# Differential attention: 24 projection pieces in the first 16 steps, score tiles three ahead from step 20

## What is computed

```
q, k, v = split(x @ w_qkv)                 # per head: two queries and keys of 64, a value of 128
q, k = partial_rotary(q) * 64 ** -.5, partial_rotary(k)
s = einsum('bqhcd,bkhcd->bhcqk', q, k)     # c = 0, 1; masked by chunks of 64
p = softmax(s)
a = p[:, :, 0] - lam * p[:, :, 1]
o = einsum('bhqk,bkhe->bqhe', a, v)
out = (rms_norm(o, g_sub) * (1 - lam_init)) @ w_o
```

## Time and profile before

| | |
|---|---|
| median of 3 runs | 2364.1 us (2362.1 to 2365.77) |
| the profiled execution | 2361.91 us, of which its span 2360.2 us |
| PE busy | 2289.7 us, 97% of the span |
| PE weight load, DVE, ACT, POOL busy | 83%, 54%, 43%, 33% |
| mean granted clock of PE | 0.995 |
| the attention loop, 32 steps | 1266.5 to 1410.7 us |

### The profile page before, as it was taken

One profiled execution on the slowest core, in us unless ns is written; L12 is line 12 of the kernel. 1 busy time (PEld: TensorE's weight loads), 2 busy tenths in 40 slices (PEclk: granted clock), 3 DMA queues, 4 the chain that ended last, 5 costly groups with the idle time before them and its releaser, 6 DMA issues. The chain is left out here.

```text
span 2360.2 us, 37346 instructions
## 1 busy us (share of the span) xinstructions
PE 2289.7 (97%) x14848; PEld 1954.7 (83%) x14848; DVE 1282.4 (54%) x2110; ACT 1020.1 (43%) x1690; POOL 775.0 (33%) x571
## 2 busy tenths in 40 slices
PE   9999999999999999999999989999999999999998
PEld 7877877878868878887887658999988888999986
DVE  6444246245635545544225774877754344777754
ACT  4345435143444543345434553554524323544522
POOL 3423344134420025333333413111254454111264
PEclk9999999999999999999999999999999999999999
DMA  5333222132210014432222212233223323233232
GB/s 153 72 72 72 82 90 89 36 81 77 89 54 3 3 38 98 90 72 54 83 89 72 72 37 72 90 107 107 93 105 106 107 89 108 90 108 107 89 107 89
DMA packets 137038, 191.96 MB, mean 81 GB/s; under 512 B 31024, under 2 KB 84656, under 8 KB 136896
## 3 DMA queue, kind: packets, MB, share of 16 engines
q1 hardware_dynamic: 128928, 183.64, 26.3%
q10 hardware_dynamic: 7968, 6.32, 0.9%
HBM read 187.84 MB, written 2.10 MB: 80 GB/s over the span
## 5 line engine op out<-in xcount | busy, mean ns | idle before, releaser
L823 POOL TENSOR_TENSOR weights_low<-weights_raw,weights_high 128x512 fp32r<-128x512 f32 x520 | 705.6, 1388 | 1205.6 <-ACT weights_high L1982 1205.6
L1982 ACT ACTIVATE weights_high<-weights_raw 128x1024 fp32r<-128x1024 f32 x260 | 260.9, 1050 | 384.3 <-PE bank L902 379.3
L900 PE MATMUL bank<-xt_high,weights_high 128*128 128x256 f32 (+1 forms) x1152 | 390.3, 339 | 3.9 <-ACT third_sum L2304 1.6
L902 PE MATMUL bank<-xt_high,weights_low 128*128 128x256 f32 (+1 forms) x1152 | 381.6, 331 | 0.0
L901 PE MATMUL bank<-xt_low,weights_high 128*128 128x256 f32 (+1 forms) x1152 | 381.0, 331 | 0.0
L900 PEld LDWEIGHTS bank<-xt_high,weights_high 128*128 128x128 f32 x1152 | 219.1, 190 | 30.7 <-POOL weights_low L823 4.9
L902 PEld LDWEIGHTS bank<-xt_high,weights_low 128*128 128x128 f32 x1152 | 218.9, 190 | 21.2
L901 PEld LDWEIGHTS bank<-xt_low,weights_high 128*128 128x128 f32 x1152 | 219.3, 190 | 16.6
L900 PE MATMUL bank<-weights_high,xt_high 128*128 128x512 f32 x432 | 173.7, 402 | 5.4 <-DVE xt_low L2869 2.8
L902 PE MATMUL bank<-weights_high,xt_low 128*128 128x512 f32 x432 | 168.8, 391 | 0.0
L901 PE MATMUL bank<-weights_low,xt_high 128*128 128x512 f32 x432 | 168.5, 390 | 0.0
(11 more groups left out here) (487 smaller groups left out, 4860.6 us busy)
## 6 DMA issues: line engine op xcount, KB each, us to landing
weights_raw<-in_fox_w_in_dram SPq DMA_DIRECT2D x64, 512.0 KB, 5.6
weights_raw<-in_ffn_w_gate_dram SPq DMA_DIRECT2D x44, 512.0 KB, 4.0
weights_raw<-in_ffn_w_up_dram SPq DMA_DIRECT2D x44, 512.0 KB, 5.0
weights_raw<-in_ffn_w_down_dram SPq DMA_DIRECT2D x40, 512.0 KB, 4.3
weights_raw<-in_gla_w_in_dram SPq DMA_DIRECT2D x24, 512.0 KB, 4.3
weights_raw<-in_gdn_w_in_dram SPq DMA_DIRECT2D x24, 512.0 KB, 4.5
weights_raw<-in_attn_w_qkv_dram SPq DMA_DIRECT2D x24, 512.0 KB, 4.5
weights_raw<-in_conv_w_in_dram SPq DMA_DIRECT2D x24, 512.0 KB, 4.3
```

The lines of the kernel that those rows point to most:

```text
L823: pool.tensor_tensor(w_lo[:, odd, k], raw[:, odd, k], w_hi[:, odd, k].bitcast(F32), ALU.subtract)\
L900: pe.matmul(out_ap, lh, rh, start=first, stop=False, skip_group_check=skip)
L902: return pe.matmul(out_ap, ll, rh, start=False, stop=last, skip_group_check=skip)
L1982: act.activation(w_hi[:, odd, 2 * m:2 * m + 2], raw[:, odd, 2 * m:2 * m + 2], ACT.Copy)\
```

## The change

The 24 pieces are dealt out anew: step n gets pieces 3n/2 to 3(n+1)/2 (rounded down), so even steps 0 to 14 have one, odd steps 1 to 15 have two, and steps 16 to 31 none. The first piece of a step stays ahead of the turning, a second one stands between the turning and the scores. `DEEP` goes from 26 to 20: step 18 issues the scores of 20 and 21, later steps are three ahead. ACT's copies and conversions and DVE's rotations follow the pieces, one step behind as before; with two pieces in a step they are done in the order of the pieces. ACT's copy of a head's output comes, from step 21 on, in the first instead of the second step behind the head (heads 4 and 5, as head 6 before).

```diff
--- before.py
+++ after.py
@@ -56,14 +56,13 @@
 PAIRED = ((0, 0), (1, 0), (0, 1), (1, 1), (2, 0), (3, 0), (2, 1), (3, 1))
 
 
-def head_piece(n):
-
-    if n < 24:
-        return 3 + n // 8, n // 2 % 4, n % 2
-    return None
-
-
-DEEP = 26
+def head_pieces(n):
+
+    units = [(p, pos, odd) for p in (3, 4, 5) for pos in range(4) for odd in range(2)]
+    return units[3 * n // 2:3 * (n + 1) // 2]
+
+
+DEEP = 20
 
 
 def score_slot(n):
@@ -1615,11 +1614,13 @@
                         pe.wait_ge(diff["v_taken"], 6 + 2 * n)
                         pair_scores(n)
                     for n in range(n_all):
-                        if head_piece(n):
-                            head_block(*head_piece(n))
+                        for unit in head_pieces(n)[:1]:
+                            head_block(*unit)
                         if n >= DEEP:
                             weigh_values(n - 1)
                         turn_pair(n)
+                        for unit in head_pieces(n)[1:]:
+                            head_block(*unit)
                         if n <= DEEP - 2:
                             pair_scores(n + 2)
                         if DEEP - 2 <= n < n_all - 3:
@@ -2491,8 +2492,7 @@
                         pair_exponentials(n)
                         if n:
                             take_pair(n - 1)
-                        if n and head_piece(n - 1):
-                            p, pos, odd = head_piece(n - 1)
+                        for p, pos, odd in head_pieces(n - 1) if n else ():
                             if odd:
                                 take_head(p, pos)
                             if pos == 3:
@@ -3370,8 +3370,9 @@
                         mix(n)
                         if DEEP <= n < n_all - 2:
                             pair_max(n + 2)
-                        if n and head_piece(n - 1) and head_piece(n - 1)[2]:
-                            rotate(*head_piece(n - 1)[:2])
+                        for p, pos, odd in head_pieces(n - 1) if n else ():
+                            if odd:
+                                rotate(p, pos)
                         if n % TT == 0 and n >= 2 * TT:
                             sum_heads(n // TT - 2)
                     sum_heads(6)
```

## The result

| | before | after |
|---|---|---|
| median of six runs each | 2364.6 us (2362.1 to 2366.7) | 2375.2 us (2370.3 to 2376.9) |
| ratio, 95% interval | | 1.0043 [1.0032, 1.0054] |
| the profiled execution | 2361.9, span 2360.2 | 2370.3, span 2368.6 |
| mean granted clock of PE in the whole of it | 0.995 | 0.993 |
| first turning of the loop to its last | 137.4 | 147.4 |

What follows compares the result with a forecast made beforehand. PE, busy in 97% of the span, was taken to bound the kernel, so only its waits count: 20.0 us come and 10.5 go, +9.5, for a median of 2373.5 us; the 8-in-10 range was 2365.5 to 2378.5.

Steps and rivals of the forecast that it cites:

- Waits for the mix: PE's waits in the loop for DVE's mixed probabilities: all but step 0's first one go, 9.0 us saved.
- (a): Refill of panel 4's second half: piece 9 waits for POOL's split of its fourth quarter; 2.0 us to come.
- (b): Step 9: the weighing waits for head 1's output copy, behind a conversion on ACT; net 1.1 us, between 0 and 1.4.
- (c): Piece 17, panel 5's second half: waits for a late conversion and POOL's split; 3.5 us, from 2.0 to 4.4.
- (d): Turning of step 16: its mix follows the max of tile 17, beside POOL; wait 1.7 us, 0.9 to 2.5.
- (e): Turning of step 17: the old jam again, last rotation in POOL's second split; wait 5.6 us, between 3.8 and 5.8.
- (f): PE's slow clock behind the jam at step 17's turning: 1.1 us as in the kernel before, from 0 to 2.
- (g): Steps 17 and 18, still two ahead with wider tiles: 4.0 us each against 1.92; 4.0 us to come, 2.2 to 4.4.
- (h): Steps 20 to 24 at 2.1 us instead of 1.92: 1.0 us to come, from 0.5 to 2.
- No collision of DVE and POOL: Rival: the packed rotations fall between POOL's splits; +3.6 us, 2367.7; chance 0.20.
- the refills keep ahead: Rival: POOL has each half's fourth quarter before the new panel's piece, so not slower; -4.1 us, 2360.0; chance 0.10.
- The low clock: Rival: PE's clock stays at half through steps 17 to 19; 3 us more, +12.5 in all, 2376.6; chance 0.15.

Runs made afterwards that it cites:

- the late split: Changed kernel with ACT's conversions of the next weights, and so POOL's split, moved from step 16 to steps 19 and 24: 2372.5 us, ratio 1.0039.
- the run with filler: Changed kernel plus matmuls whose result nobody reads, ahead of the turnings of steps 16, 17 and 18 while PE waits: 2370.1 us, ratio 1.0030.
- filler in the kernel before: Kernel before plus 70 idle matmuls ahead of the turning of step 25, inside its 5.10 us wait: 2363.1 us, ratio 0.9993.

## Why the prediction was right, and where it was not

The forecast was 2373.5 (+9.5), and the median is 2375.2; the loop of the profiled execution is 10.0 longer. Direction, place and size held. The parts of the sum did less well, and that the total came out so close is in part luck, as their errors cancelled. Of the signs named, the weighing of step 9 (1.47), the jam at the turning of step 17 (4.39, the rotation at 1.64), 2.07 a step afterwards and the longer loop are in the trace; the gap in piece 9 and the second one behind the jam are smaller than announced (0.9 and 0.89). A ledger by stretch, with a piece at 2.86: from the turning of step 0 to that of step 16 the kernel before takes 77.15 and does 16 pieces, the changed one 101.62 and does 23, so without the seven more 24.47 - 20.02 = 4.45 come. From there to the turning of step 31 it is 60.24 and 45.73, or +5.51. The price of a piece matters here: the steps 1 to 3, in which neither kernel waits, take 13.56 with three pieces and 19.05 with five, or 2.75 a piece, and at that price the two stretches give +5.3 and +4.7. The total is 10.0 either way.

- *Waits for the mix, 9.0 to go:* right. No turning of steps 1 to 15 waits any more.
- *(a) piece 9, 2.0:* 0.9. The step that failed is POOL's duration: I let it lie near 6.38, and it took 5.01, under the 5.45 of my lower bound, as did two splits around the loop's start in the kernel before (5.03 and 5.04).
- *(b) the weighing of step 9, net 1.1:* 1.47 against a usual 0.27, so 1.2. What I left out is that two other such waits of the earlier trace rows within the packed steps vanish, 0.5 of gain.
- *(c) piece 17, 3.5:* 4.0, by the way foretold (rotation, head copy, conversion, split). The run with ACT's order changed shows that the same time is lost, mostly a step earlier, when the conversion comes first.
- *(d) the turning of step 16, 1.7:* 2.54, just over the upper bound of 2.5. Two of the mix's operations took 1.7 more beside POOL. The run with the late split takes 1.7 of it away.
- *(e) the jam, 7.6 from turning to turning:* 7.51. The number is right, its parts are not: the wait was 4.39, not 5.6, since PE's own work took 3.1, not 2.0, most of it at half clock. POOL's part, which I took over from the old jam, is shown by the late split: 2.2 of the step.
- *(f), (g) behind it:* mis-sized by the most. I had 4.0 for each of steps 17 and 18 and 1.1 for the clock; they took 5.28 and 5.29, and step 19, which I had at 1.9, took 4.88. At full clock, in the run with filler, they take 4.01, 3.94 and 3.18. So (g) was right for steps 17 and 18, the transition in step 19 costs 1.3 that I didn't see, and the clock 4.3 where I had 1.1.
- *What I didn't credit:* the old end. I took away its waits and its slow clock, but counted its own work at 1.92 a step. Without their waits, steps 23 and 24 of the kernel before took 2.23 and 3.62 (3.01 - 0.78, 8.72 - 5.10), as step 24 has two score tiles to make. That is 2.0 which the change moves to step 18, and I counted it there as new.
- *(h), 1.0:* 10.15 for steps 20 to 24, 0.55 over 1.92 each.

From step 16 on I had +3.4 behind that step's own wait, and it was +4.7 to +5.5, by the two prices of a piece: 4.4 too little for steps 17 to 19, 2.0 too much for the old end. Up to step 16 I had +6.1 with (d), and it was +4.5 to +5.3. The parts measured there add up to 5.9, so 0.6 or more of a gain in that stretch stays unexplained.

*The rivals.* No collision of DVE and POOL is refuted by the trace and by the late split. That the refills keep ahead is refuted by piece 17. The low clock was called a rival at 0.15, and its condition came true in the profiled execution: steps 17 to 19 at 0.50. It didn't come out at its +12.5 there, for the two reasons above ((a) smaller, old end not credited); the median of the runs lies between it and the forecast. Steps 26 to 31 of the old kernel, which I held against it, were three ahead; the new steps were two ahead, with gaps of 2.5, 4.4, 1.7 and 0.9. And I had read only 1.6 us of the old low stretch, which was four times as long. What the profile after doesn't show in full is why the other runs took 3.2 to 6.5 us more than the profiled one. Up to 4.4 us can come from the code ahead of the loop, where the profiles of this case differ by that much and the profile after is the earliest of all. Their mean clock is lower (0.990 to 0.991 for 0.993), and in profiles of the related kernels the clock also fell in the starved step 11 and at the loop's end, but there is no profile of such a run of this kernel; that stays argued.

## What to carry to other kernels

A wait that goes because its step gets more cover comes back where the cover was taken: sum both ends, with the old end's own work credited, before you call a packing a gain. Work that is pushed out of a jam (a rotation, a conversion, a neighbour's split) keeps its price if the steps it goes to are no looser: none of the moves tried here (rotation, ACT's order, conversion and split) made its kernel faster beyond the intervals. Price a thin stretch at both levels of PE's clock: here that was the largest term that the forecast had too small.

## What the hardware showed that I had not expected

- In the profile after PE kept half clock for some 20 us (1372.4 to 1392.8), through stretches in which it worked 3.56 of 5.30, 4.41 of 5.30 and 2.90 of 2.90 us, and came back only in step 19.
- Executions of one kernel differ in where the clock falls, and their times go with its mean: 2367.3 to 2368.6 at 0.997 and 2373.5 to 2374.9 at 0.992 with filler in the changed kernel; with filler in the kernel before, one at 0.999 took 2358.0 where those at 0.995 to 0.996 took 2363.0 to 2364.2. Filler in one place doesn't keep the clock elsewhere (0.79 in the starved step and 0.66 at the loop's end beside 1.00 where the filler stood).
- A two-input operation of DVE on one column, 0.22 by itself, takes 0.96 beside POOL, more than four times as long, so even the shortest of them must be priced by its neighbour.
